# Transposed residual in two chunk places instead of four, one expert load in the room that this frees

## The chip, the cores and the metric

The kernel runs on one core of a Trainium2 chip. The metric is the time of one execution on the device in microseconds, as the median of several runs.

## The reference

One layer of a hybrid backbone for two streams of 128 tokens (context and latent), D = 2048, all in 32-bit floats. What matters here is its second half: the merged branches go through one output projection, the result is added to the residual (x1), the router's logits are taken from the normalised and modulated x1, and every token goes to the best 2 of 4 experts in its best of 4 groups.

```
x1 = x + ga1 * (merged @ w_out)                 # merged: sigmoid-gated sum of the two branches
h2 = rmsnorm(x1, norm2_g) * (1 + sc2) + sh2
lg, lf = h2 @ w_rg + b_rg, h2 @ w_re + b_re     # 4 group logits, 16 expert logits
# top group, then top 2 of its 4 experts, weights comb from the two softmaxes
for e in range(16):
    y = y + comb[:, e:e+1] * ((silu(h2 @ w_g[e]) * (h2 @ w_u[e])) @ w_d[e])
out = rmsnorm(x1 + ga2 * y, final_norm_g)
```

The weights are some 400 MB, and every byte of them is read once.

## The kernel before

The work is a row of stages on one core, each engine with its own hand-written program, synchronised by semaphores. In the dense stages a weight load of 1 MB (512 rows by 512 columns) goes into one of four slots `raw`; ScalarE rounds it into `w_hi` (`high`, L1362), VectorE takes the rest `w_lo` (`low`, L1719), and TensorE multiplies each of its two halves (`unit`, L812, 12 matmuls: two streams, two row blocks, three products). `w_hi` and `w_lo` hold four units (`AHEAD`, L32). A load is numbered l; loads L_OUT to L_ALL-1 (L344, L345, sixteen of them) are the output projection. It makes four column chunks of x1, numbered 24 to 27, with four loads each. A chunk's sums lie in banks 0 and 1 (chunks 25 and 27) or 2 and 3 (chunks 24 and 26; `banks_of`, L394).

When a chunk's last unit is used, VectorE reads it (`read_chunk`, L1810): for each stream a product with the gate (L1850) and a sum into `x1` (L1856). Behind the second product `step.settle()` waits for it, and only then is `chunk_read` raised (L1854); `reads(chunk)` (L399) is its value when that chunk has been read. TensorE transposes each stream's x1 columns (`x1_transposes`, L1010), stream 0 behind load l = L_OUT+4, +8, +12 and stream 1 in the middle of load +6, +10, +14; the last chunk's two come after the last load. ScalarE copies the transposed columns into `x1T` (`x1_transposed`, L1520), which has four chunk places, 16 KB in each partition. From it TensorE multiplies the router's weights (`router`, L1020, 4 products of 20 columns for one chunk and stream, which the profile shows as 8 matmuls at L1027); all of them sum into banks 2 and 3, so the first one waits until chunk 26 has been read (L1023). The products of chunk 0 stand in load L_ALL-3, those of chunk 1 in L_ALL-2, the others behind the last load (L1050 to L1079, L1098 to L1103).

The expert stage reads 1 MB pieces of the expert weights. SP issues them in a fixed order into a ring of eleven slots, eight of which lie where `w_hi`, `w_lo` and `raw` were; four more places are used once (loads 12 to 15, `slab`, L442). Two of these, `mraw_f[0]` and `mraw_f[1]` for loads 13 and 14, lie in the same 16 KB as `x1T`. So SP issues them only when all router products are done (`route_done`, L591). Before that SP issues loads 9, 10 and 8 at the start of the output projection, 15 when load L_ALL-3 has been used (L583), and 0, 2, 1, 3, 12 and 4 as the dense slots come free. From the second pair of experts on, each load waits until TensorE has used the slot (`slot_free`, L538, wait at L546). The first pair's gate and up loads are 0 to 15. During the output projection ScalarE's own queue issues the `w_out` loads (`dense_load`, L486, L499) and the last four loads of w_ada (L483).

Of the kernel before, what the change touches and what calls it, by code (L numbers as in the profile page):

```python
# [8 lines left out]
ACT = mybir.ActivationFunctionType  # L9
# [4 lines left out]
P = 128  # L14
TOK = 128
NS = 2
D = 2048
KD = D // P
# [6 lines left out]
NG, EPG, NE, EH = 4, 4, 16, 512  # L25
# [95 lines left out]
def backbone_step(nc, x_prompt, x_sample, cache_k, cache_v, c, c_ctx, norm1_g, norm2_g, w_ada, b_ada,  # L121
# [24 lines left out]
    with ExitStack() as ctx:  # L146
# [6 lines left out]
        def place(name, shape, offset, dt=F32):  # L153
            return nc.alloc_sbuf_tensor_at(name, shape, dt, offset=offset).ap()
# [8 lines left out]
        KB = 1024  # L163
# [9 lines left out]
        A, F, B = region(32 * KB), region(32 * KB), region(16 * KB)  # L173
# [13 lines left out]
        o_lo = place("o_lo", [P, KF, NS, TOK], F + 24 * KB, F32R)  # L187
        x1 = place("x1", [P, NS, D], F)
        ga2b = place("ga2b", [P, NS, D], F + 16 * KB)
        x1T = place("x1T", [P, KD, NS, TOK], F + 16 * KB)  # L190

        xg = place("xg", [P, KD, EPG * CAP], A)
        row_hi = place("row_hi", [P, COL], A + 14 * KB, F32R)
# [43 lines left out]
        gw = place("gw", [P, NS, KD, NG + NE], C + 4 * (C_DFTN + 384))  # L237
# [38 lines left out]
        bank = [ctx.enter_context(nc.psum_tensor(f"bank{i}", [P, COL], F32)) for i in range(8)]  # L276
# [7 lines left out]
        hi_ready, unit_used = sem("hi_ready"), sem("unit_used")  # L284
# [114 lines left out]
        def reads(chunk):  # L399

            return chunk + 1 + 3 * P0_CHUNKS

        def x1T_bank(n, s):

            return 4 + (2 * n + s) % 3
# [99 lines left out]
        @block.sync  # L505
        def _(sp):
            for s in range(NS):
                sp.dma_start(x0[:, s], x_v[s]).then_inc(x_in, 16)

            def ada_block_load(b, j):  # L510

                n = 8 * b + j
                if n >= ARAW:
                    sp.wait_ge(ada_done, n - ARAW + 1)
                for m in (SHIFT1, SCALE1):
                    sp.dma_start(araw[:, n % ARAW, 2 * m:2 * m + 2],
                                 ada_v[:, 2 * j:2 * j + 2, m * D + b * COL:m * D + (b + 1) * COL]).then_inc(part_landed[n % ARAW], 16)

            for j in range(8):
                ada_block_load(0, j)  # L520
            dense_load(sp, 0)
            for b in range(1, BLOCKS):
                for i in range(P0_CHUNKS):
                    if i < 4:
                        ada_block_load(b, 2 * i)
                        ada_block_load(b, 2 * i + 1)
                    dense_load(sp, P0_CHUNKS * (b - 1) + i + 1)
            for l in range(L_LOOP, SP_DENSE - 1):
                if l < L_LAST_ADA - LATE_ADA:
                    ada_super_load(sp, A_SUPER + l - L_LOOP)  # L530
                dense_load(sp, l + 1)

            def expert_load(n, view, row, col):

                sp.dma_start(slab(n).rearrange("p (a m) -> p a m", a=1),
                             view[:, row:row + 1, col:col + D]).then_inc(landed(n), 16)

            def slot_free(r, n):  # L538

                place = place_in_ring(n)  # L540
                if place >= MRAW:
                    sp.wait_ge(loads_used, used_value(r, load_at(place - MRAW)))
                else:
                    last = range(place, LOADS - ONCE, MRAW)[-1]
                    sp.wait_ge(loads_used, used_value(r - 1, load_at(last)))
                sp.sem_inc(slots_freed, 1)  # L546

            def gate_up_loads(r, i, q, up):
                for x in range(PAIR):
                    n = 2 * gate_up_unit(i, q, up) + x  # L550
                    slot_free(r, n)
                    expert_load(n, (gate_v, up_v)[up], i * PAIR + x, q * LOAD_K * COL)

            def down_loads(r, i):
                for k in range(KE):
                    for x in range(PAIR):
                        n = 2 * down_unit(i, k) + x
                        slot_free(r, n)
                        expert_load(n, down_v, (i * PAIR + x) * KE + k, 0)

            def last_down_loads(r):

                for q in range(D // COL):
                    for half in range(2):
                        n = 2 * down_unit(PAIRS - 1, q) + half
                        slot_free(r, n)
                        for x in range(PAIR):
                            row = ((PAIRS - 1) * PAIR + x) * KE + 2 * half
                            sp.dma_start(slab(n)[:, 2 * x * COL:(2 * x + 2) * COL].rearrange("p (k m) -> p k m", k=2),
                                         down_v[:, row:row + 2, q * COL:(q + 1) * COL]).then_inc(part_landed[2 * q + half], 16)  # L570

            rounds_end = sp.alloc_register("rounds_end")
            sp.reg_mov(rounds_end, 1)
            with sp.Fori(0, rounds_end) as r:

                def first_gate_up_load(n):
                    expert_load(n, (gate_v, up_v)[n // 2 % 2], n % 2, n // 4 * LOAD_K * COL)

                first_gate_up_load(9)
                first_gate_up_load(10)  # L580
                sp.wait_ge(chunk_read, reads(21))
                first_gate_up_load(8)
                sp.wait_ge(unit_used, 2 * L_ALL - 4)  # L583
                first_gate_up_load(15)
                for n in (0, 2, 1, 3):
                    sp.wait_ge(unit_used, 2 * L_ALL - 2 + n % 2 * 2)
                    first_gate_up_load(n)
                first_gate_up_load(12)
                sp.wait_ge(raw_done[0], 8 * (RING_LOADS // RAW))
                first_gate_up_load(RAW)  # L590
                sp.wait_ge(route_done, NS)  # L591
                first_gate_up_load(13)
                first_gate_up_load(14)
                for n in range(1, RAW):
                    sp.wait_ge(raw_done[n], 8 * (RING_LOADS // RAW))
                    first_gate_up_load(RAW + n)
                sp.wait_ge(rounds_ready, 1)
                sp.reg_load(rounds_end, rounds[0:1, 0:1])
                slot_free(r, 11)
                first_gate_up_load(11)  # L600
                for i in range(1, PAIRS):
                    for q in range(2):
                        for up in range(2):
                            gate_up_loads(r, i, q, up)
                    down_loads(r, i - 1)
                    for q in (2, 3):
                        for up in range(2):
                            gate_up_loads(r, i, q, up)
                last_down_loads(r)

                sp.wait_ge(x2_squared, r * 8 + 8)
                sp.sem_inc(slots_freed, 1)
                for place in range(MRAW):
                    slot_free(r + 1, load_at(place))

            sp.wait_ge(y_ready_act, 1)
            sp.dma_start(y_v[0][:, 0:2 * COL], x1[:, 0, 0:2 * COL]).then_inc(out_sent, 16)
            for s in range(NS):
                sp.wait_ge(y_ready, s + 1)
                sp.dma_start(y_v[s][:, 2 * COL:4 * COL], x1[:, s, 2 * COL:4 * COL]).then_inc(out_sent, 16)  # L620
            sp.wait_ge(out_sent, 16 * NS * 2)
            sp.wait_ge(kv_sent, 32)
# [159 lines left out]
        def _(pe):  # L782
# [237 lines left out]
            def router(n, s):  # L1020

                if n == 0:
                    pe.wait_ge(chunk_read, reads(26))  # L1023
                    pe.wait_ge(gw_ready, 1)
                pe.wait_ge(x1T_ready, 2 * n + s + 1)
                for k in range(4 * n, 4 * n + 4):
                    last = nc.tensor.matmul(bank[2 + s][:, 0:NG + NE], x1T[:, k, s], gw[:, s, k],  # L1027
                                            start=k == 0, stop=k == KD - 1)
                return last

# [7 lines left out]
            for l in range(L_LOOP, L_ALL - 1):  # L1038
# [8 lines left out]
                if l > L_LOOP:  # L1047
                    for a in supers_at(l):
                        ada_super(a)
                if l == L_ALL - 3:  # L1050
                    router(0, 0)
                if l == L_ALL - 2:
                    router(1, 0)
                for h in range(HEADS):
# [18 lines left out]
                        ada_super(a)  # L1073
                if l > L_OUT and l % 4 == 0:
                    x1_transposes((l - L_OUT) // 4 - 1, 0)
                if l == L_ALL - 3:
                    router(0, 1)
                if l == L_ALL - 2:
                    router(1, 1)  # L1079
                if l == ROUTER_AT + 2:  # L1080
# [279 lines left out]
        def _(act):  # L1360
# [158 lines left out]

            def x1_transposed(n, s):  # L1520
                act.wait_ge(x1T_done, 2 * n + s + 1)
                nc.scalar.activation(x1T[:, 4 * n:4 * n + 4, s], bank[x1T_bank(n, s)][:].rearrange("p (k t) -> p k t", k=4), ACT.Copy
                                     ).then_inc(x1T_ready, 1)

            def permuted(x, s, n):
# [779 lines left out]
```

## Time and profile before

| | us |
|---|---|
| median of 3 runs | 1196.16 |
| the runs | 1195.09 to 1196.16 |
| the profiled execution | 1196.65 |
| its span, first to last instruction | 1194.8 |
| TensorE busy in it | 1116.9 (93%) |
| VectorE busy | 535.9 (45%) |
| ScalarE busy | 366.3 (31%) |
| DMA, mean rate over the span | 354 GB/s |

A page of the profile gives the busy time of each engine, the span in 40 equal slices, and the chain of work that ended last. TensorE is busy 93% of the span, and 27% of the chain is DMA; both are means over stages with different limits, so the stretches of the stages that the change touches have to be read one by one. In the rows "PE" is TensorE, "DVE" VectorE, "ACT" ScalarE, "SP" the engine that issues most loads, and "PEclk" or the number behind the busy times the share of the full TensorE clock that was granted.

### The profile page before, as it was taken

The page shows a single profiled execution, that of the slowest core. Times are in us where ns is not written, and L with a number is a line of the kernel's source. Part 1 is how long each engine was busy: PE and PEld are TensorE (multiplying, and loading weights), DVE is VectorE, ACT ScalarE, POOL GpSimd, SP SyncE. Part 2 cuts the span into 40 slices and gives each one's busy share as a digit, 9 for nine tenths or more (in the row PEclk, how much of TensorE's full clock was granted, in tenths as well). Part 3 has the DMA queues.
Part 4 walks back from the last instruction along what each step waited for, and adds up shares of the span by engine and source line. Part 5 has one row for each costly group of instructions (what it writes and reads, how often), then busy time and mean ns, then how long its engine had stood idle before and what let it go on. Part 6 is the DMA issues. An engine that isn't in the chain of part 4 may idle for free.

```text
span 1194.8 us, 14481 instructions
## 1 busy us (share of the span) xinstructions
PE 1116.9 (93%) x5577; PEld 682.5 (57%) x5577; DVE 535.9 (45%) x781; ACT 366.3 (31%) x526; POOL 54.8 (5%) x100
## 2 busy tenths in 40 slices
PE   5899999999999999999999999999999888988795
PEld 2566766777777677667788875434344234423231
DVE  0464575555455444454466755242416041504056
ACT  3342342444433333333345533320112001201023
POOL 0210200110000220000010100000000000000000
PEclk9999999999999999999999999999999999999997
DMA  9999978887877898888898799999999999999994
GB/s 357 385 386 381 364 286 320 312 302 281 286 289 283 306 351 323 326 299 319 329 362 260 219 381 423 390 415 423 423 423 423 423 422 424 422 423 423 423 406 174
DMA packets 114964, 423.22 MB, mean 354 GB/s; under 512 B 9088, under 2 KB 9264, under 8 KB 82640
## 3 DMA queue, kind: packets, MB, share of 16 engines
q1 hardware_dynamic: 101968, 389.57, 83.4%
q0 software_dynamic: 5424, 15.35, 4.8%
q10 hardware_dynamic: 7504, 17.37, 4.0%
q8 instruction: 45, 0.74, 0.2%
q14 instruction: 23, 0.19, 0.0%
HBM read 418.27 MB, written 3.98 MB: 353 GB/s over the span
## 4 chain that ended last, share of the span: by engine, by line
PE 69%; DMA 27%; SPq 1%; DVE 1%; issue 1%; ACT 1%; DVEq 0%
PE bank L827 14%; PE bank L828 13%; PE bank L829 13%; PE bank L1196 10%; DMA mraw<-in_w_exp_up 10%; DMA mraw<-in_w_exp_down 5%; PE bank L808 5%; DMA raw<-in_w_in 4%; DMA mraw<-in_w_exp_gate 4%; PE bank L1235 3%; DMA raw<-in_w_ada 2%; PE bank L1135 2%; DMA mraw_y<-in_w_exp_gate 2%; PE bank L792 1%; PE bank L1277 1%; PE bank L1258 1%
## 5 line engine op out<-in xcount | busy, mean ns | idle before, releaser
L1724 DVE TENSOR_TENSOR w_lo<-raw,w_hi 128x1024 fp32r<-128x1024 f32 x192 | 231.8, 1223 | 246.7 <-ACT w_hi L1370 245.6
L1370 ACT ACTIVATE w_hi<-raw 128x1024 fp32r<-128x1024 f32 x192 | 200.3, 1057 | 313.3 <-DMA raw<-in_w_in 160.4
L827 PE MATMUL bank<-w_hi,h_hi 128*128 128x512 f32 x512 | 206.2, 403 | 6.6 <-DVE w_lo L1724 4.3
L828 PE MATMUL bank<-w_lo,h_hi 128*128 128x512 f32 x512 | 200.1, 391 | 0.0
L829 PE MATMUL bank<-w_hi,h_lo 128*128 128x512 f32 x512 | 199.8, 390 | 0.0
L1196 PE MATMUL bank<-mraw,xg 128*64 128x512 f32 x720 | 184.9, 597 | 12.5 <-DMA mraw<-in_w_exp_gate 4.8
L827 PEld LDWEIGHTS bank<-w_hi,h_hi 128*128 128x128 f32 x512 | 96.2, 188 | 47.1 <-issue 24.8
L1196 PEld LDWEIGHTS bank<-mraw,xg 128*64 128x64 f32 x720 | 57.7, 136 | 108.4 <-issue 105.6
L829 PEld LDWEIGHTS bank<-w_hi,h_lo 128*128 128x128 f32 x512 | 96.1, 188 | 21.0
L828 PEld LDWEIGHTS bank<-w_lo,h_hi 128*128 128x128 f32 x512 | 96.3, 188 | 18.1
L2190 DVE SCALAR_TENSOR_TENSOR d_lo<-bank,slot_w,d_hi 128x512 fp32r<-128x512 f32 x32 | 23.9, 747 | 161.6 <-ACT d_hi L1669 161.0
L1235 PE MATMUL bank<-mraw,hidT 128*64 128x512 f32 x336 | 84.3, 607 | 12.2 <-DMA mraw<-in_w_exp_down 12.2
L1669 ACT ACTIVATE d_hi<-bank,slot_w 128x512 fp32r<-128x512 f32 x32 | 22.0, 688 | 226.8 <-PE bank L1235 142.3
L2202 DVE TENSOR_TENSOR bank<-bank,ga2b 128x512 f32<-128x512 f32 x64 | 41.5, 694 | 77.1 <-PE bank L1277 77.0
L808 PE MATMUL bank<-raw,cpad 128*32 128x512 f32 x512 | 63.3, 610 | 2.8 <-DMA raw<-in_w_ada 2.8
L1235 PEld LDWEIGHTS bank<-mraw,hidT 128*64 128x64 f32 x336 | 26.9, 139 | 57.2 <-issue 52.7
L792 PE MATMUL bank<-araw,cpad 128*32 128x512 f32 x256 | 34.2, 643 | 14.8 <-DMA araw<-in_w_ada 14.8
L827 PE MATMUL bank<-w_hi,m_hi 128*128 128x512 f32 x120 | 47.7, 398 | 0.0
L829 PE MATMUL bank<-w_hi,m_lo 128*128 128x512 f32 x120 | 46.9, 390 | 0.0
L828 PE MATMUL bank<-w_lo,m_hi 128*128 128x512 f32 x120 | 46.7, 390 | 0.0
L2129 DVE TENSOR_TENSOR xg<-bank,rbi 128x512 f32<-128x512 f32 x32 | 21.9, 684 | 52.8 <-PE bank L1135 52.8
L1196 PE MATMUL bank<-mraw_g,xg 128*64 128x512 f32 x96 | 43.7, 598 | 1.6 <-DMA mraw_x<-in_w_exp_up 1.2
(293 smaller groups left out, 1332.2 us busy)
## 6 DMA issues: line engine op xcount, KB each, us to landing
raw<-in_w_in SPq DMA_DIRECT2D x64, 1024.0 KB, 8.3
raw<-in_w_ada SPq DMA_DIRECT2D x60, 1024.0 KB, 8.2
mraw<-in_w_exp_gate SPq DMA_DIRECT2D x46, 1024.0 KB, 20.8
mraw<-in_w_exp_up SPq DMA_DIRECT2D x44, 1024.0 KB, 20.9
mraw<-in_w_exp_down SPq DMA_DIRECT2D x42, 1024.0 KB, 20.6
araw<-in_w_ada SPq DMA_DIRECT2D x64, 512.0 KB, 10.9
raw<-in_w_out ACTq DMA_DIRECT2D x12, 1024.0 KB, 9.3
raw<-in_w_na_o SPq DMA_DIRECT2D x8, 1024.0 KB, 7.2
```

Source lines behind the costliest of these rows:

```text
L792: last = nc.tensor.matmul(bank[7 - b % 2][32 * g:32 * g + 32], cpad[:, 2 * j + g % 2], araw[:, n % ARAW, g], start=j == 0, stop=j == 7)
L808: last = nc.tensor.matmul(bank[7][32 * g:32 * g + 32], cpad[:, k], raw[:, n % RAW, g], start=k == 0, stop=k == KD - 1)
L827: nc.tensor.matmul(o, hi[:, k, s], wh, start=k == first, stop=False)
L828: nc.tensor.matmul(o, hi[:, k, s], wl, start=False, stop=False)
L829: last = nc.tensor.matmul(o, lo[:, k, s], wh, start=False, stop=k == final)
L1135: last = nc.tensor.matmul(out[:, kk * EPG * CAP:(kk + 1) * EPG * CAP], (t_hi, t_lo)[part][:, s, k * P:(k + 1) * P], pick[:, s, g * EPG:(g ...
L1196: last = nc.tensor.matmul(out[x * CAP:(x + 1) * CAP], xg[:, q * LOAD_K + kk, e * CAP:(e + 1) * CAP], slab(2 * unit + x)[:, kk * COL:(kk + ...
L1235: last = nc.tensor.matmul(bank[first_bank + n][x * CAP:(x + 1) * CAP], hidT[:, i % 2, k, x * CAP:(x + 1) * CAP], slab(2 * unit + x)[:, n * ...
L1370: nc.scalar.activation(w_hi[:, u % AHEAD], r, ACT.Copy).then_inc(hi_ready, 1)
L1724: v.tensor_tensor(w_lo[:, u % AHEAD], r, w_hi[:, u % AHEAD].bitcast(F32), ALU.subtract).then_inc(raw_done[n % RAW], 4)
L2190: v.scalar_tensor_tensor(out=d_lo[:, c % 2], in0=bank[first_bank + n][:], scalar=slot_w[:, i:i + 1], in1=d_hi[:, c % 2].bitcast(F32), op0= ...
L2202: v.tensor_tensor(bank[out + s][:], bank[out + s][:], ga2b[:, s, cols], ALU.mult).then_inc(y_scaled, 1)
```

## The change

`x1T` gets two chunk places instead of four. Chunk n uses place n mod 2, so chunk 2 goes where chunk 0 lay. The products of chunk 0 are therefore put one load earlier, into load L_ALL-4, both streams between that load's two units, in front of the transposes of chunk 2 behind the second unit. The freed 8 KB are the place of load 14; SP issues it behind two waits of its own (chunk 22 read, and unit 14 of the output projection used) before load 15, and no longer behind `route_done`.

```diff
@@ -187,7 +187,7 @@
         x1 = place("x1", [P, NS, D], F)
         ga2b = place("ga2b", [P, NS, D], F + 16 * KB)
-        x1T = place("x1T", [P, KD, NS, TOK], F + 16 * KB)
+        x1T = place("x1T", [P, 2 * 4, NS, TOK], F + 16 * KB)
@@ -580,6 +580,9 @@
                 first_gate_up_load(10)
                 sp.wait_ge(chunk_read, reads(21))
                 first_gate_up_load(8)
+                sp.wait_ge(chunk_read, reads(22))
+                sp.wait_ge(unit_used, 2 * L_OUT + 14)
+                first_gate_up_load(14)
                 sp.wait_ge(unit_used, 2 * L_ALL - 4)
                 first_gate_up_load(15)
@@ -590,7 +593,6 @@
                 first_gate_up_load(RAW)
                 sp.wait_ge(route_done, NS)
                 first_gate_up_load(13)
-                first_gate_up_load(14)
@@ -1024,7 +1026,7 @@
                 for k in range(4 * n, 4 * n + 4):
-                    last = nc.tensor.matmul(bank[2 + s][:, 0:NG + NE], x1T[:, k, s], gw[:, s, k],
+                    last = nc.tensor.matmul(bank[2 + s][:, 0:NG + NE], x1T[:, k % 8, s], gw[:, s, k],
                                             start=k == 0, stop=k == KD - 1)
@@ -1047,8 +1049,9 @@
-                if l == L_ALL - 3:
+                if l == L_ALL - 4:
                     router(0, 0)
+                    router(0, 1)
                 if l == L_ALL - 2:
                     router(1, 0)
@@ -1073,8 +1076,6 @@
                 if l > L_OUT and l % 4 == 0:
                     x1_transposes((l - L_OUT) // 4 - 1, 0)
-                if l == L_ALL - 3:
-                    router(0, 1)
                 if l == L_ALL - 2:
                     router(1, 1)
@@ -1519,7 +1520,7 @@
                 act.wait_ge(x1T_done, 2 * n + s + 1)
-                nc.scalar.activation(x1T[:, 4 * n:4 * n + 4, s], bank[x1T_bank(n, s)][:].rearrange("p (k t) -> p k t", k=4), ACT.Copy
+                nc.scalar.activation(x1T[:, n % 2 * 4:n % 2 * 4 + 4, s], bank[x1T_bank(n, s)][:].rearrange("p (k t) -> p k t", k=4), ACT.Copy
                                      ).then_inc(x1T_ready, 1)
```

## Rows read from the trace of the kernel before

**Rows 1.** Stretches: us, busy time (instructions) of each engine, PEclk, DMA share, GB/s.

```profile
680.00:690.00 10.00, 10.00 (x54) 8.43 (x52) 7.17 (x9) 4.71 (x8) 2.13 (x4) 1.00 0.65 171
690.00:715.00 25.00, 24.37 (x152) 18.13 (x151) 13.95 (x34) 9.42 (x19) 0.00 (x0) 0.93 1.00 403
...
757.00:760.00 3.00, 3.00 (x16) 1.01 (x14) 0.69 (x1) 1.24 (x2) 0.00 (x0) 1.00 0.76 259
...
774.00:778.00 4.00, 4.00 (x23) 1.82 (x24) 2.58 (x4) 0.00 (x0) 0.00 (x0) 1.00 0.88 289
...
782.00:830.00 48.00, 48.00 (x236) 19.98 (x234) 18.50 (x29) 8.20 (x16) 0.00 (x0) 1.00 1.01 423
830.00:1170.00 340.00, 303.57 (x1399) 122.08 (x1397) 105.19 (x166) 45.40 (x86) 0.00 (x0) 0.99 1.01 421
```

**Rows 2.** Waits of SP's queue, 715 to 782 us: total, times, longest.

```profile
SPq L546 <- PE bank L1196: 47.8, 10, 10.2
SPq L546 <- PE bank L1235: 7.2, 2, 4.7
```

**Rows 3.** Chain that ended last, in order of time: start, us, what.

```profile
686.10 0.80 PE bank L1027 x8
...
829.77 15.40 DMA mraw<-in_w_exp_up
```

**Rows 4.** SP's expert load issued at 778.5 us, alone, and its time to landing.

```profile
L535 SPq DMA_DIRECT2D mraw_x<-in_w_exp_up x1: 328/328/328, 778.5 to 778.5; - x1
...
DMA to landing us min/median/max: 6.2/6.2/6.2
```

**Rows 5.** Tile raw on ScalarE, 649.4 to 677.6 us; landings of its six loads.

```profile
L499 ACTq DMA_DIRECT2D raw<-in_w_out x5: 374/374/375, 649.3 to 672.1; - x5
L483 ACTq DMA_DIRECT2D raw<-in_w_ada x1: 353/353/353, 677.5 to 677.5; - x1
...
  PE bank L829: 14.1, 10
...
DMA to landing us min/median/max: 4.7/6.8/10.0
```

**Rows 6.** ScalarE in order of time: start, us, what [idle before, releaser].

```profile
663.47 1.06 ACT L1370 ACTIVATE w_hi<-raw 128x1024 fp32r<-128x1024 f32 x1 [0.77 <-PE bank L829]
```

**Rows 7.** TensorE in order of time, the first matmuls of both units of L_OUT+12.

```profile
677.30 0.39 PE L827 MATMUL bank<-w_hi,m_hi 128*128 128x512 f32 x1
...
680.02 0.39 PE L827 MATMUL bank<-w_hi,m_hi 128*128 128x512 f32 x1
```

**Rows 8.** VectorE in order of time, around the reading of chunk 26.

```profile
678.67 1.23 DVE L1724 TENSOR_TENSOR w_lo<-raw,w_hi 128x1024 fp32r<-128x1024 f32 x1 [1.44 <-ACT w_hi L1370]
...
681.13 0.68 DVE L1850 TENSOR_TENSOR gab<-gab,bank 128x512 f32<-128x512 f32 x1
681.96 0.69 DVE L1856 TENSOR_TENSOR x<-x,gab 128x512 f32<-128x512 f32 x1 [0.15 <-DVE gab L1850]
```

**Rows 9.** VectorE and TensorE in order of time, two handoffs between them.

```profile
71.97 1.23 DVE L1724 TENSOR_TENSOR w_lo<-raw,w_hi 128x1024 fp32r<-128x1024 f32 x1 [5.24 <-ACT w_hi L1370]
...
73.34 0.47 PE L827 MATMUL bank<-w_hi,h_hi 128*128 128x512 f32 x1 [1.22 <-DVE w_lo L1724]
...
715.09 0.70 PE L1146 MATMUL bank<-pick,rr 128*128 128x256 f32 x4 [0.71 <-DVE pick L2111]
```

**Rows 10.** TensorE in order of time, behind three pauses.

```profile
39.27 0.50 PE L827 MATMUL bank<-w_hi,h_hi 128*128 128x512 f32 x1 [2.17 <-DVE h_lo L1758]
...
1014.40 5.35 PE L1235 MATMUL bank<-mraw,hidT 128*64 128x512 f32 x16 [2.05 <-DMA mraw<-in_w_exp_down]
...
1069.48 3.65 PE L1235 MATMUL bank<-mraw,hidT 128*64 128x512 f32 x16 [1.41 <-DMA mraw<-in_w_exp_down]
```

**Rows 11.** TensorE's stretches: us, busy (matmuls), granted clock, DMA share, GB/s.

```profile
40.00:42.00 2.00, 2.00 (x10) 1.00 1.04 384
...
708.00:709.00 1.00, 1.00 (x7) 0.50 1.00 418
...
1015.00:1018.00 3.00, 3.00 (x10) 0.50 1.00 418
```

## The prediction, as it was made

> **What bounds the kernel now.** I read the stretches first, then each engine's order of time in the output stage, then the loads of the expert stage. The stretches [rows 1] show three regimes. Between 680 and 690 us TensorE is busy without a break while the DMA engines have room: 171 GB/s, against 421 to 423 GB/s where they are full. From 690 us they are nearly full, but TensorE still has hardly a gap. From 782 us to 1170 us the DMA engines stay at full rate and TensorE has holes (303.57 us busy of 340). So moving bytes forward helps only if the full-rate stretch begins or ends earlier.
>
> The stretch in between decides that. At 757 to 760 us and 774 to 778 us the rate falls to 259 and 289 GB/s [rows 1], although more than 380 us of transfers at full rate are still to come. The DMA queue's own waits say why [rows 2]: between 715 and 782 us it waits 47.8 us for L1196 and 7.2 us for L1235, TensorE's expert matmuls. All slots are full, and a load is issued only when TensorE has used up an old one. In the chain of waits the first link behind 686 us that is a transfer is issued at 829.77 us [rows 3]; it took 15.40 us because loads stood queued before it. The row to look at is the last load that found nearly nothing queued: issued at 778.5 us, landed 6.2 us later [rows 4]. After it the queue does not run dry again. So the end is set by when TensorE frees a slot at 778.5 us, plus a fixed amount of transfer. It is not set by how many loads were done before.
>
> **The change, part by part.**
>
> Load 14 forward. It leaves its place behind the routing and is issued when the units of the out projection's seventh load are used (`2 * L_OUT + 14`). One load is 1.05 MB, 2.48 us at 423 GB/s. If every byte in front of the end counted, this would be the gain. But the loads behind it then land 2.48 us earlier, the slots are full 2.48 us earlier, and the queue is dry for longer at 757 and 774 us, because the next issues still wait for TensorE. What is left of the gain is the part of the 6.2 us that the load of 778.5 us spent behind earlier ones. Of six loads of the same size on ScalarE's queue the fastest landed in 4.7 us [rows 5], so up to 6.2 - 4.7 = 1.5 us can be saved. Bounds: 0 (it stands behind just as much) and 2.48 us (C, below). I take 1.0 us, nearer to the full 1.5 because the queue will be drier than it was. The Trainium skill (DMA: Bandwidth & Descriptors, "Anatomy of one DMA") gives about 2.0 us fixed plus the bytes at 436 GB/s, for the GpSimd path: an estimate of 4.4 us for this load. No row here is as low; by it the saving would be up to 1.8 us and the sum 0.8 us lower.
>
> Load 14 in the output stage. Its 2.48 us run beside the w_out loads on ScalarE's queue. The slowest of those six landed in 10.0 us [rows 5]; even at 10.0 + 2.48 the one issued at 649.3 us would land at 661.8 us, and ScalarE reads that slot from 663.47 us [rows 6]. I take 0; without this cover the cost is at most 2.48 us. On SP's queue the two new waits stand in front of load 15 alone, which waits for a later unit anyway: 0. The issue that falls away behind the routing was no bottleneck, since the queue soon waits for slots [rows 2]: 0.
>
> x1T halved. The same eight copies and the same transposes: 0. Chunk 2 now goes where chunk 0 lay, and on TensorE, which works in order, the products of chunk 0 now stand before the transposes of chunk 2: no new wait there.
>
> The router products one load earlier. The two groups of eight small matmuls for chunk 0, 0.80 us each [rows 3], only move. But `router(0, 0)` waits at L1023 until chunk 26 is read out of banks 2 and 3. Today TensorE reaches it at 686.10 us, long after. Now both groups stand between the two units of load L_OUT+12 = L_ALL-4: the first begins at 677.30 us, the second at 680.02 us [rows 7]. VectorE reads chunk 26 [rows 8] right behind the `low` of 678.67 us; its second product runs from 681.13 to 681.81 us. The signal goes out behind `step.settle()`, and VectorE's next instruction starts at 681.96 us. From VectorE's end to TensorE's next matmul another handoff took 0.14 us (a `low` from 71.97 us for 1.23 us, the matmul at 73.34 us, [rows 9]). So TensorE stands still from 680.02 to about 682.10 us: 2.1 us. Bounds: 1.8 us (the wait ends with the product at 681.81) and 2.6 us (the slowest handoff near by left TensorE idle for 0.71 us, [rows 9]; 681.96 + 0.71 - 680.02). Queued behind it on TensorE is everything that follows: the second unit, the transposes of chunk 2, the last loads, the routing, the gathers. Nothing takes the pause up. TensorE has no gap there to give [rows 1], ScalarE is the one that waits for TensorE (14.1 us in ten waits, [rows 5]), and so does SP. So the slot of 778.5 us is freed 2.1 us later.
>
> The clock behind the pause. Before 1014.40 us TensorE idled 2.05 us. Soon after it resumed, the granted clock fell to 0.50, that is 1.2 GHz, and 16 matmuls took 5.35 us against 3.65 us at full clock, 1.70 us more [rows 10, 11]. A pause of 2.17 us before 39.27 us had no such result: 1.00 behind it [rows 10, 11]. So a pause of this length can go either way. Here the 2.1 us are followed at once by 1.6 us of products with 20 columns, and such light work does not hold the clock up: at 708 us it stood at 0.50 [rows 11] behind the last products. So I expect the fall. It would lie over dense units for the most part, so I price it like the row, +1.7 us, with bounds 0 and 1.7. The Trainium skill (TensorE: Matmul & The Clock Gate, "What's actually happening") says that a monitor halves the clock of an array that was lately idle. By that rule the sum is the one below, without it 1.7 us less; the row of 1014.40 us agrees, the row of 39.27 us does not.
>
> Sum: +2.1 + 1.7 - 1.0 = +2.8 us. The profiled execution took 1196.65 us (1194.8 us span, 1.85 us outside it); the median of the runs is 1196.16 us, 0.49 us lower. The terms are differences, so I add them to the median: **1199.0 us**, +0.23%.
>
> **The rivals.**
> A, the pause without the fall of the clock: +2.1 - 1.0 = +1.1, 1197.3 us. For it: the row of 39.27 us. Against: the pause and the light products together last 3.7 us.
> B, the forecast: 1199.0 us.
> C, the load is worth its full 2.48 us at the end because the queue behind 757 us is not really dry: 1195.8 us with the pause, 1197.5 us with the clock's fall too. For it: in the dips the rate is only some 35% down, so some DMA engines were behind others. Against: 6.2 us to landing.
> D, the other side, faster: no pause. If VectorE has read chunk 26 before TensorE arrives, only the load's gain is left: 1195.2 us at -1.0, 1193.7 us at the full -2.48. It decides if the product that ends at 681.81 us ends before 680.02 us, that is, if VectorE ran 1.8 us ahead. Against: the `low` in front of it waits for ScalarE [rows 8], and ScalarE for TensorE [rows 5], so VectorE cannot run ahead.
> That load 14 is not issued early at all would leave +2.1 or +3.8 us, inside B's and A's ranges; its wait is met five and a half loads before 680 us, at two units of 2.72 us each [rows 7] about 30 us, so it gets no chance of its own.
>
> **How the numbers follow.** Chances: B 0.60, A 0.24, C 0.10, D 0.06. B spans 1.8 + 1.7 - 1.5 to 2.6 + 1.7 - 0, so 1198.2 to 1200.5 us; A, likewise, 1196.5 to 1198.8 us. The range of 1196.3 to 1200.4 us holds both and the slower part of C; D and the rest of C are left out. A measurement of this kernel can tell about 0.2%, 2.4 us, from no change: below 1193.8 us is faster, above 1198.55 us slower. Faster is most of D: 0.05. Slower is B but for its lowest part, and a little of A: 0.57. The rest is 0.38.
>
> **What would show it.** Right: in the profile after, TensorE idles about 2 us before the first product at L1027, near 680 us, released by VectorE's L1850; load 14 is issued near 649 us; the dips of the DMA rate near 760 and 776 us are deeper; the load behind the second dip lands in about 5 us; the granted clock is 0.50 for some microseconds near 685 us (B) or not (A). Wrong: no idle time there (D), no dips behind 757 us (C), or a w_out load that lands later than ScalarE reads it.

## The result, and the profile after

The changed kernel took 1201.85 us (median of 5 runs, 1201.3 to 1202.3), against 1196.16 us (5 runs, 1195.09 to 1196.32) for the kernel before on the same chip: 1.0047 times, 95% interval 1.0033 to 1.0060, or 5.69 us more. The prediction said 1199.0 us with a range up to 1200.4 us. The direction was right; the size was twice what was forecast, and the time lies outside the range. The profiled execution took 1202.30 us (span 1200.5 us), 5.65 us above the one of before. Its lines are shifted by one or two (products L1029 for L1027, transposes L1019 for L1017, the units L829 to L831 for L827 to L829, VectorE's product L1851 for L1850), and its origin by 0.16 us: what lay at 680.02 us before lies at 680.18 us here if nothing has changed.

TensorE after, in order of time, from the end of the first unit of load L_OUT+12 on; start, us, what, idle before and its releaser (answers to [rows 3, 7]):

```profile
679.95 0.39 PE L831 MATMUL bank<-w_hi,m_lo 128*128 128x512 f32 x1
682.08 2.75 PE L1029 MATMUL bank<-gw,x1T 128*128 128x20 f32 x16 [1.74 <-DVEq L1855]
684.66 0.77 PE L829 MATMUL bank<-w_hi,m_hi 128*128 128x512 f32 x1
685.24 0.63 PE L830 MATMUL bank<-w_lo,m_hi 128*128 128x512 f32 x1
...
689.50 0.57 PE L831 MATMUL bank<-w_hi,m_lo 128*128 128x512 f32 x1
689.91 0.60 PE L1019 MATMUL bank<-cst_all,x 128*128 128x128 f32 x4
690.27 0.48 PE L829 MATMUL bank<-w_hi,m_hi 128*128 128x512 f32 x1
...
698.54 0.96 PE L1029 MATMUL bank<-gw,x1T 128*128 128x20 f32 x8
```

VectorE after, around the reading of chunk 26 (answers to [rows 8]):

```profile
680.68 0.69 DVE L1857 TENSOR_TENSOR x<-x,gab 128x512 f32<-128x512 f32 x1
681.29 0.68 DVE L1851 TENSOR_TENSOR gab<-gab,bank 128x512 f32<-128x512 f32 x1
682.12 0.69 DVE L1857 TENSOR_TENSOR x<-x,gab 128x512 f32<-128x512 f32 x1 [0.15 <-DVE gab L1851]
```

The pause is there, where it was predicted: TensorE stands until VectorE's second product has ended at 681.97 us. The slowing behind it was predicted too, but it is larger than the price that the prediction gave it. The 16 small products take 2.58 us to the start of the next matmul, against two groups of 0.80 us [rows 3]. The twelve matmuls of the second unit follow each other every 0.43 us, not 0.23 us, and fill 5.25 us, against the 2.72 us that a unit takes in [rows 7].

Stretches after, with the columns of [rows 1]:

```profile
680.00:690.00 10.00, 8.26 (x31) 6.67 (x30) 4.96 (x8) 1.06 (x1) 2.12 (x4) 0.66 0.70 164
...
757.00:760.00 3.00, 3.00 (x18) 0.95 (x16) 0.00 (x0) 0.53 (x2) 0.00 (x0) 1.00 1.00 421
...
774.00:778.00 4.00, 4.00 (x20) 1.34 (x19) 2.18 (x4) 3.24 (x7) 0.00 (x0) 1.00 1.00 414
778.00:782.00 4.00, 4.00 (x26) 2.58 (x28) 2.68 (x4) 0.00 (x0) 0.00 (x0) 1.00 0.88 336
```

The mean granted clock of 680 to 690 us is 0.66, where it was 1.00. The clock has two levels here, 1.00 and 0.50, so 0.34 below full means 2 * 0.34 * 10 = 6.8 us at 0.50, that is 1.2 GHz. Single microseconds show that it lay in one piece (TensorE alone: us, busy, granted clock, DMA share, GB/s; answers to [rows 11]), and the two last lines show that the first dip of the DMA rate has moved and is deeper than the 259 GB/s of [rows 1]:

```profile
683.00:684.00 1.00, 1.00 (x7) 0.53 0.00 0
686.00:687.00 1.00, 1.00 (x4) 0.50 1.07 180
689.00:690.00 1.00, 1.00 (x4) 0.56 0.99 164
...
761.00:764.00 3.00, 3.00 (x16) 1.00 0.29 120
764.00:774.00 10.00, 10.00 (x60) 1.00 0.99 398
```

The second dip has moved as well (336 GB/s at 778 to 782 us), but it is shallower than the 289 GB/s of [rows 1], against the sign that the prediction named.

The delay can be added up on TensorE. The first product of chunk 1 began in the kernel before, TensorE in order of time, at:

```profile
693.28 0.96 PE L1027 MATMUL bank<-gw,x1T 128*128 128x20 f32 x8
```

From 680.02 us to there it is 13.26 us, and after (680.18 to 698.54) it is 18.36 us, 5.10 us more, with the same work in between. The pause is 682.08 - 680.18 = 1.90 us of it. The products take 2.58 - 2 * 0.80 = 0.98 us more and the second unit 5.25 - 2.72 = 2.53 us more. The remaining -0.3 us is the difference in the rest of the stretch, where products no longer stand between the other units. These 5.10 us pass to the end as they are. SP's queue in order of time (start, us, what), the load of the slot that decides and the ninth load behind it, first of the kernel before:

```profile
778.50 0.33 SPq L535 DMA_DIRECT2D mraw_x<-in_w_exp_up  x1
...
792.75 0.33 SPq L535 DMA_DIRECT2D mraw<-in_w_exp_gate  x1
```

The same two of the kernel after:

```profile
783.69 0.33 SPq L535 DMA_DIRECT2D mraw_x<-in_w_exp_up  x1
...
797.93 0.33 SPq L535 DMA_DIRECT2D mraw<-in_w_exp_gate  x1
```

And each of the two of after read alone, with its time to landing (answer to [rows 4]):

```profile
L535 SPq DMA_DIRECT2D mraw_x<-in_w_exp_up x1: 328/328/328, 783.7 to 783.7; - x1
...
DMA to landing us min/median/max: 7.4/7.4/7.4
...
L535 SPq DMA_DIRECT2D mraw<-in_w_exp_gate x1: 328/328/328, 797.9 to 797.9; - x1
...
DMA to landing us min/median/max: 15.4/15.4/15.4
```

Without the shift of the origin the slot comes free 783.69 - 778.50 - 0.16 = 5.03 us later, the ninth load behind it is issued 5.02 us later, and takes 15.4 us to land in both kernels. The load of the slot itself took 7.4 us, not the 6.2 us of [rows 4], and not the 5 us that the prediction hoped for. The early load 14 has left nothing at this point.

### The profile page after: what moved, and what is told of

It is laid out like the page before. It is cut to its first block, busy times and chain, and to the rows that moved or that the text cites. A ratio compares the mean times of both kernels' runs of the same rounds, so it can differ in the third digit from the quotient of the medians.

```text
span 1200.5 us, 14482 instructions
## 1 busy us (share of the span) xinstructions
PE 1118.6 (93%) x5577; PEld 683.9 (57%) x5577; DVE 536.2 (45%) x781; ACT 366.3 (31%) x526; POOL 54.6 (5%) x100
## 4 chain that ended last, share of the span: by engine, by line
PE 69%; DMA 27%; DVE 1%; SPq 1%; issue 1%; ACT 1%; DVEq 0%
PE bank L829 14%; PE bank L830 13%; PE bank L831 13%; PE bank L1197 11%; DMA mraw<-in_w_exp_up 10%; PE bank L810 5%; DMA raw<-in_w_in 4%; DMA mraw<-in_w_exp_gate 3%; DMA mraw<-in_w_exp_down 3%; PE bank L1236 2%; PE bank L1136 2%; DMA raw<-in_w_ada 2%; DMA mraw_y<-in_w_exp_gate 2%; DMA araw<-in_w_ada 2%; PE bank L1278 1%; PE bank L794 1%
## 5 line engine op out<-in xcount | busy, mean ns | idle before, releaser
L829 PE MATMUL bank<-w_hi,h_hi 128*128 128x512 f32 x512 | 206.2, 403 | 7.7 <-DVE w_lo L1725 5.0
L831 PE MATMUL bank<-w_hi,h_lo 128*128 128x512 f32 x512 | 199.8, 390 | 0.0
L829 PEld LDWEIGHTS bank<-w_hi,h_hi 128*128 128x128 f32 x512 | 96.2, 188 | 48.2 <-issue 25.4
L831 PEld LDWEIGHTS bank<-w_hi,h_lo 128*128 128x128 f32 x512 | 96.1, 188 | 21.0
L829 PE MATMUL bank<-w_hi,m_hi 128*128 128x512 f32 x120 | 48.6, 405 | 0.0
L831 PE MATMUL bank<-w_hi,m_lo 128*128 128x512 f32 x120 | 47.7, 398 | 0.0
```

The source lines that it names most:

```text
L829: nc.tensor.matmul(o, hi[:, k, s], wh, start=k == first, stop=False)
L831: last = nc.tensor.matmul(o, lo[:, k, s], wh, start=False, stop=k == final)
```

## Experiments

All times are medians; the kernel before, run in between on the same chip, stood at 1196.2 us (e1 to e4), 1196.3 us (e5 to e8) and 1196.0 us (e9 to e11).

**e1: the early products without the pause.** Both groups of products move behind the second unit, directly ahead of the transposes of chunk 2, so that chunk 26 has been read when TensorE arrives.

```diff
-                if l == L_ALL - 4:
-                    router(0, 0)
-                    router(0, 1)
...
+                if l == L_ALL - 4:
+                    router(0, 0)
+                    router(0, 1)
```

> The changed kernel with both product groups of chunk 0 behind the second unit of load L_ALL-4, directly in front of the transposes of chunk 2. TensorE gets there at about 682.9 us, VectorE has read chunk 26 at about 682.0 us, so the pause should be gone. Theory (the time is pause plus half clock; the load forward is worth nothing at the end, since the end hangs on the slot freed near 778 us): 1196.2 us, between 1195.2 and 1197.0. Rival L (the load forward is worth its 2.48 us and something else costs the more): 1193.7 us. Rival T (load 14's traffic in the output stage costs the time): about 1201 us, as in the changed kernel.

1196.55 us (12 runs), 1.0002 times the kernel before (0.9993 to 1.0010). In its trace there is no pause and no fall of the clock at this place. TensorE in order of time:

```profile
682.09 1.85 PE L1029 MATMUL bank<-gw,x1T 128*128 128x20 f32 x16
```

The stretch around it, with the columns of [rows 1]:

```profile
680.00:690.00 10.00, 10.00 (x56) 8.59 (x56) 6.55 (x8) 4.20 (x8) 2.13 (x4) 1.00 0.58 170
```

The place of the products is the whole loss: 1201.85 - 1196.55 = 5.3 us. Everything else in the change, load 14 among it, nets to nothing within the interval.

**e2: load 14 back behind the routing,** everything else as changed.

```diff
-                sp.wait_ge(chunk_read, reads(22))
-                sp.wait_ge(unit_used, 2 * L_OUT + 14)
-                first_gate_up_load(14)
...
                 first_gate_up_load(13)
+                first_gate_up_load(14)
```

> The changed kernel with load 14 back behind the routing; x1T halved and the products early, as changed. Theory: the load's place is worth nothing at the end: 1201.8 us, as the changed kernel, within 0.7. Rival L (worth 2.48 us): 1204.3 us. Prediction's term (worth 1.0 us): 1202.8 us. Rival T (the load costs about 3 us where it is now): 1199 us.

1201.26 us, 1.0034 times (1.0021 to 1.0047): no later than with the early load. Pause and fall are those of the changed kernel (1.74 us idle, mean clock 0.66 from 680 to 690 us).

**e3: the pause filled.** Nine matmuls of 512 columns, about 2 us, into a free bank stand ahead of the products; TensorE reaches them as late as before, but has not idled. The nine results are not used.

```diff
                 if l == L_ALL - 4:
+                    for i in range(9):
+                        nc.tensor.matmul(bank[5][:].rearrange("p (k s t) -> p k s t", k=2, s=NS), m_hi[:, i, 0], m_hi[:, 4:6],
+                                         start=True, stop=True)
                     router(0, 0)
```

> The changed kernel with nine extra matmuls of 512 columns (9 x 0.227 = 2.05 us, into the free bank 5, never read) where TensorE waits for chunk 26. The wait is filled with dense work of the same length. Theory (idle time drew the clock down): granted clock 1.00 near 685 us, TensorE later by 2.0 us instead of 5.1, time 1198.2 us. Rival P (the light products alone draw it down): clock 0.50 for some time behind 683 us, 1199.9 us. Rival S (the shift has nothing to do with the clock): 1201.8 us.

1198.66 us, 1.0016 times (1.0006 to 1.0025). The products begin within 0.14 us of the changed kernel's, but take 1.86 us, and the clock stays up. TensorE in order of time, the nine matmuls, the products and the first product of chunk 1:

```profile
680.18 2.21 PE L1054 MATMUL bank<-m_hi 128*128 128x512 f32 x9
682.22 1.86 PE L1029 MATMUL bank<-gw,x1T 128*128 128x20 f32 x16
...
695.41 0.96 PE L1029 MATMUL bank<-gw,x1T 128*128 128x20 f32 x8
```

The stretch around it, with the columns of [rows 1]:

```profile
680.00:690.00 10.00, 10.00 (x56) 8.50 (x55) 6.20 (x9) 3.46 (x6) 2.13 (x4) 1.00 0.69 162
```

Nearly the same delay of the products, no fall: 1201.85 - 1198.66 = 3.2 us is the price of the fall. The traces agree: from the end of the first unit to the first product of chunk 1 it is 15.23 us here, against 13.26 us before and 18.36 us after, so the fall alone is worth 3.13 us on TensorE.

**e4: the pause alone.** The kernel before, with the wait for chunk 26 put between the two units of that load and the products left where they were.

```diff
+                if l == L_ALL - 4:
+                    pe.wait_ge(chunk_read, reads(26))
```

> The kernel before with one added wait: TensorE waits for chunk 26 between the two units of load L_ALL-4, and the products stay one load later, where they were; x1T whole, load 14 late. The pause is alone, dense units stand behind it. Theory: a pause of 1.9 us; if the clock holds 1198.1 us; if it falls, less long than the 6.8 us of the changed kernel, since dense work follows at once: 1199.8 us. Rival (products and pause have nothing to do with each other, the clock falls as long as before): 1201.5 us.

1198.82 us, 1.0021 times (1.0011 to 1.0031), so 1.3 to 3.7 us. TensorE idles as long as in the changed kernel, then dense units follow, and in its trace the clock does not fall here. TensorE in order of time, from the last matmul of the first unit to the first product of chunk 1:

```profile
679.58 0.39 PE L829 MATMUL bank<-w_hi,m_lo 128*128 128x512 f32 x1
681.70 0.50 PE L827 MATMUL bank<-w_hi,m_hi 128*128 128x512 f32 x1 [1.74 <-DVEq L1856]
...
695.11 0.96 PE L1027 MATMUL bank<-gw,x1T 128*128 128x20 f32 x8
```

The stretch around it, with the columns of [rows 1]:

```profile
680.00:690.00 10.00, 8.30 (x42) 7.01 (x43) 6.63 (x9) 4.51 (x7) 2.13 (x4) 1.00 0.50 140
```

Matmuls of a unit start 0.23 us apart, so the first unit ends at 679.81 us. Counted from there TensorE is 15.30 us away from chunk 1's products, 2.0 us more than before.

So neither the pause (e4) nor the light products (e1, e3) bring the clock down here. Both together do. Each of these is one trace: e1's is of a run of 1199.70 us, e4's of one of 1197.58 us, neither of them near its median. The mean granted clock that is on record for every run says the same: it averages 0.9928 over the 12 runs of e1, 0.9927 over the 12 of e3 and 0.9928 over the 11 of e4, as over 29 runs of the kernel before (0.9928), but 0.9898 over the five runs each of the changed kernel and of e2. By 2 * 0.0030 * 1200 that is 7.2 us at half clock, close to the 6.8 us of the trace.

**e5: one group of products between the units,** the other behind the second unit.

```diff
                 if l == L_ALL - 4:
                     router(0, 0)
-                    router(0, 1)
...
+                if l == L_ALL - 4:
+                    router(0, 1)
```

> The changed kernel with only the first product group of chunk 0 between the units (behind the wait for chunk 26) and the second one behind the second unit. The pause stays, the light work behind it is halved to 0.8 us. Theory (pause and light work together keep the clock down for 6.8 us): half clock shorter than in the changed kernel or absent; pause 1.9 plus 0 to 1.7: 1198.2 to 1199.9 us. Rival (any product behind the pause is enough): 1201.6 us, as the changed kernel.

1199.97 us, 1.0027 times (1.0013 to 1.0040). The same pause, half the light work behind it. TensorE in order of time:

```profile
681.97 1.07 PE L1029 MATMUL bank<-gw,x1T 128*128 128x20 f32 x8 [1.74 <-DVEq L1856]
```

The stretch around it, with the columns of [rows 1]:

```profile
680.00:690.00 10.00, 8.26 (x40) 6.86 (x40) 6.08 (x8) 3.45 (x6) 2.13 (x4) 0.83 0.67 159
```

A mean of 0.83 is 2 * 0.17 * 10 = 3.4 us at half clock, half of the changed kernel's 6.8 us. That is the length that the prediction had taken for two groups. It is one trace, and the nine runs lie between 1197.3 and 1202.7 us, where the five of the changed kernel lie within 1.0 us. That the length goes with the number of products is therefore not shown.

**e6: a load held back.** In the kernel before, load 15 is issued behind the routing, after 13 and 14, rather than when load L_ALL-3 has been used.

```diff
-                first_gate_up_load(15)
...
                 first_gate_up_load(14)
+                first_gate_up_load(15)
```

> The kernel before with one more load held back: load 15 is issued behind the routing, behind loads 13 and 14, and no longer when load L_ALL-3 is used. Between 690 and 710 us one load less moves (2.48 us). Theory (the end hangs on TensorE's slot near 778 us, the number of loads done before counts for nothing): 1196.2 us, or up to 1.3 us more if the dips at 757 and 774 us close. Rival L (every load in front counts): 1198.7 us.

1199.31 us, 1.0016 times (1.0006 to 1.0026): 0.7 to 3.1 us slower. The theory's plain case, no change, is out; its 1.3 us for closed dips and the rival's 2.5 us both lie in the interval. It is not the clock alone: among the runs with a mean granted clock of 0.993 or 0.994 six of e6 average 1198.0 us and nineteen of the kernel before 1196.0 us. In its trace the slots come free on the timetable of the kernel before (table below). But the ninth load behind the third slot, issued 73.1 us after the first expert matmul as in the kernel before, takes 1.3 us longer to land than the 15.4 us there:

```profile
L535 SPq DMA_DIRECT2D mraw<-in_w_exp_gate x1: 327/327/327, 795.0 to 795.0; - x1
...
DMA to landing us min/median/max: 16.7/16.7/16.7
```

So one load later costs something with the slots unmoved, while one load earlier (e1 against e11, below) gains nothing. It fits a queue that in the kernel before is just short of full in the dips, 259 and 289 GB/s [rows 1]; this reason for e6 is argued, not shown.

**e7 and e8: 2 us of matmuls in the expert stage.** Nine unused matmuls of 512 columns ahead of the second pair of experts (e7, near 754 us), or ahead of the fifth (e8, `i == 4`), in the stretch where the DMA engines are full.

```diff
+                    if i == 1 and q == 0 and up == 0:
+                        for j in range(9):
+                            nc.tensor.matmul(bank[2 * (i % 2)][:], t_hi[:, 0, j * P:(j + 1) * P], t_hi[:, 1, 0:COL],
+                                             start=True, stop=True)
```

> The kernel before with nine extra matmuls of 512 columns (2.05 us, into a bank that is about to be written anew, never read) in front of the second pair's first gate product, at about 754 us, in front of the last dry spells of the DMA queue. Theory (what TensorE loses in front of 778 us passes to the end in full): 1198.2 us. Rival (the end is set by the bytes to move): 1196.2 to 1196.7 us.

> The same nine extra matmuls in front of the fifth pair's first gate product, where the DMA queue never runs dry. Theory: hidden in TensorE's waits, 1196.2 us, within 0.6. Rival (TensorE's work passes to the end wherever it stands): 1198.2 us.

e7: 1199.59 us, 1.0028 times (1.0015 to 1.0041), so 1.8 to 4.9 us. e8: 1196.37 us, 0.9996 times (0.9986 to 1.0006). The same work costs its full length before 778 us and nothing behind it. TensorE's time up to the last slot that finds the queue nearly empty is what the end is made of, as long as no load comes later than in the kernel before (e6).

**e9 and e10: the slots freed sooner.** In the first pair of experts the transposes of the picks, the ga2 rows and the gathers for later pairs move behind matmuls that free slots. e9 is e1 with this order, e10 the kernel before with it. The core of the edit on TensorE (ScalarE's copies move along):

```diff
-                        pe.wait_ge(pick_ready, r * 2 + 2)
-                        pe.wait_ge(xg_scaled, r * 32 + 6)
...
-                ga2_rows(0)
-                ga2_rows(1)
...
+                        pick_transposes()
                     gate_up(i, 1, 0)
-                    next_group(i, 0)
+                    if i == 1:
+                        ga2_rows(0)
+                        ga2_rows(1)
+                    else:
+                        next_group(i, 0)
```

> The changed kernel with the products of chunk 0 behind the second unit of load L_ALL-4, and with another order in the first pair of experts: the transposes of the gathered picks and the ga2 rows stand behind the second pair's first gate and up products, so TensorE comes sooner to the matmuls that free the expert slots. Theory (the end is set by when TensorE frees the slots around 757 to 779 us, plus a fixed amount of transfer): the slots of 757.9, 772.8 and 778.5 us come free 2.1 to 3.4 us sooner, so 2.3 us less than 1196.2: about 1194.0. Rival (the DMA engines' bytes alone set the end, the slots do not): 1196.2, no change.

> The same other order in the first pair of experts, put into the kernel before (load 14 behind the routing, four places of x1T). Theory: 1.4 to 1.7 us less than 1196.2, about 1194.6, a little less than in the changed kernel, since with earlier slots the load that is already there counts for more. Rival (the slots do not set the end): 1196.2, no change.

e9: 1193.95 us (12 runs), 0.9981 times (0.9969 to 0.9993). e10: 1194.79 us (12 runs), 0.9984 times (0.9972 to 0.9997). Both are faster than both kernels, against the one before e9 by 2.0 us and e10 by 1.2 us. Counted from the first expert matmul of each trace, three slots come free at these times, and TensorE's last matmul starts at that in the last column:

| | first expert matmul at, us | slot 1 | slot 2 | slot 3 | last matmul |
|---|---|---|---|---|---|
| before | 719.66 | 38.26 | 53.15 | 58.84 | 461.74 |
| after | 724.86 | 38.26 | 53.14 | 58.83 | 462.20 |
| e6 | 721.90 | 38.26 | 53.14 | 58.83 | 462.93 |
| e7 | 718.82 | 40.51 | 55.39 | 61.09 | 464.26 |
| e9 | 718.47 | 35.74 | 49.75 | 57.84 | 459.95 |
| e10 | 721.80 | 35.74 | 49.74 | 57.84 | 461.42 |

(In the kernel before slot 1 is refilled at 757.92 us, slot 2 at 772.81 us, and slot 3 is that of [rows 4].) The changed kernel frees its slots on the same timetable as the one before, to 0.01 us; only its start is 5.20 us late (5.04 us without the shift of the origin). The last matmul is a blunter mark than the slots: in the ten traces with this timetable (before, after, e1 to e6, e8, e11) it lies between 461.74 and 463.06 us. e7 and e9 move the timetable, and TensorE's last matmul moves beyond that scatter: against the kernel before 2.5 us later (2.25 us of it already at the slots) and 1.8 us sooner. In e10 it moves by 0.3 us only, so its gain is shown by the times of its runs alone. Its trace is of a run of 1198.46 us. Among the runs with a mean granted clock of 0.993 or 0.994 ten of e9 and eight of e10 both average 1194.0 us, and eighteen of the kernel before 1195.8 us: the order is worth 1.8 us with either place of load 14. The third slot came 1.0 us sooner, not the 2.1 us of the estimate; the first two came as estimated.

**e11: e1 with load 14 behind the routing.**

```diff
-                sp.wait_ge(chunk_read, reads(22))
-                sp.wait_ge(unit_used, 2 * L_OUT + 14)
-                first_gate_up_load(14)
...
                 first_gate_up_load(13)
+                first_gate_up_load(14)
```

> The changed kernel with the products of chunk 0 behind the second unit of load L_ALL-4, as in e1, and with load 14 issued behind the routing again; what is left of the change is two places for x1T and products that stand a little earlier. Theory (load 14's early place is worth nothing while the slots are late): the same as e1, 1196.2 to 1196.6. Rival (load 14 early is worth 1.0 us or more, hidden in e1 by a cost of the products' new place): 1197.3 or more.

1196.42 us (12 runs), 0.9998 times (0.9987 to 1.0010), against 1196.55 us of e1. The early place of load 14 is worth nothing also where TensorE is not late.

## Why the prediction missed

| term | predicted, us | measured, us | by |
|---|---|---|---|
| pause | +2.1 (1.8 to 2.6) | +1.9 | the trace after; e4 is 2.6 slower in all |
| fall of the clock | +1.7 (0 to 1.7) | +3.2 to +3.5 | after against e3; products and unit at half clock |
| load 14 forward | -1.0 (-2.48 to 0) | 0 | e2 against after: 0.6 the other way; e11 against e1: 0.1 |
| sum | +2.8 | +5.7 | medians |

The measured terms make 5.1 to 5.4 us, and TensorE's first expert matmul comes 5.0 us later. The remaining 0.3 to 0.6 us are not put down to anything; they are less than the scatter of the last matmul.

**The pause** was right, in its place, releaser and size.

**The clock was the step that failed,** by its size. That it would fall, and why there (a pause followed by light products), was right, and e1, e3 and e4 show it: take away the idle time or the light products, and it does not fall here. But the sentence that such light work does not hold the clock up says too much: without the pause 16 products left it at 1.00 (e1, e3). The fall was priced like the row of 1014.40 us, as 1.7 us, and that value was made the upper bound too. But there dense matmuls followed the pause; here 1.6 us of 20-column products did, and they were slowed themselves. In the traces the fall had the length of that row with one group of them (e5, 3.4 us at half clock), and twice that with two (6.8 us, the changed kernel and e2). The dense unit that TensorE had meanwhile took nearly twice as long. The row of 1014.40 us was a sample of one, of another kind of work, so it could be no upper bound. Of the miss of 2.85 us this term is 1.5 to 1.8 us and load 14, below, 1.0 us. With twice its price as the bound the range would have reached about 1202.1 us and held the time.

The Trainium skill (TensorE: Matmul & The Clock Gate, "What's actually happening") puts the halving down to how busy the array was lately. e3 and e5 agree with it; the trace of e4, idle for the same 1.74 us without a fall, shows that such a pause alone is not enough at this place.

**Load 14** was the second error. The prediction itself argued that a load in front of a dry queue is worth nothing, and then took 1.0 us back for a shorter time to landing behind the second dip. In the first dip this came true: the load issued at 763.1 us into an almost empty queue landed in 4.7 us, not the 6.1 us of its counterpart (757.9 us before). This load of after, read alone:

```profile
L535 SPq DMA_DIRECT2D mraw<-in_w_exp_down x1: 327/327/327, 763.1 to 763.1; - x1
...
DMA to landing us min/median/max: 4.7/4.7/4.7
```

That is the value of the fastest of [rows 5]. The Trainium skill (DMA: Bandwidth & Descriptors, "Anatomy of one DMA") makes an estimate of 4.4 us for it, by a fit for the GpSimd path; the measured 4.7 us decides. But the queue was not empty at the second dip: eight slots later the same load as in [rows 4] took 7.4 us. The gain of the first dip is used up by the next slot that TensorE has yet to free. Why this load took 1.2 us longer than before is not settled. Load 14 is not the reason, for in e2, with load 14 back behind the routing, it took 7.2 us too. At the ninth load behind it the difference is gone.

**The cover in the output stage** held: load 14 was issued at 649.55 us, and no wait of ScalarE's `high` grew; the six `raw` loads beside it landed in 4.7 to 9.9 us, against 4.7 to 10.0 us in [rows 5]. Tile raw on ScalarE's queue after:

```profile
L499 ACTq DMA_DIRECT2D raw<-in_w_out x5: 374/375/408, 649.5 to 672.2; - x5
...
  PE bank L831: 14.1, 10
...
DMA to landing us min/median/max: 4.7/7.5/9.9
```

**What bounds the kernel** was read rightly for TensorE's part, and e7 to e9 show it: the end follows TensorE's timetable up to the slots of 758 to 779 us. That the number of loads done before does not count held for a load moved forward (e2, e11), and not for one held back (e6). **Rivals.** C (the load worth its 2.48 us) fell by e2 and e11, D (no pause) by the trace after. A (no fall) fell for this kernel; e3 stands in for it, at 1198.66 us with the load gain at 0.

## What to carry over

A wait put between two dense stretches cost more than its idle time here, where the first thing behind it was light work: put the light work where its inputs are already there (e1, 5.3 us), or dense work first (in e4's trace the clock held). Price a clock fall by what runs behind the pause, and do not take the one example that a trace has for its upper bound: here it was twice that. Before moving a load forward, ask which engine frees the place of the next load: here TensorE's order of freeing the slots set the end, and reordering TensorE's work by which slot it frees gained 2.0 us (e9), where the load gained none.

## What had not been expected of the hardware

The clock also falls near 707 us, behind the last router products, and there its length differs from run to run of much the same code. TensorE alone from 700 to 720 us, with the columns of [rows 11], in the trace of before:

```profile
700.00:720.00 20.00, 19.29 (x135) 0.91 1.00 403
```

In that of e1:

```profile
700.00:720.00 20.00, 20.00 (x119) 0.74 1.00 410
```

In that of e9:

```profile
700.00:720.00 20.00, 18.77 (x140) 1.00 1.01 424
```

That is about 3.5 us, 10 us and nothing at half clock. Of the thirteen traces five have none there (e4, e5, e7, e9, e11), five have about 3.5 us (before, after, e2, e3, e8) and three about 10 us (e1, e6, e10). What sets the length there was not tried.

A pause in front of dense work is no surer. The one near 39 us [rows 10], 2.17 us with no fall in the kernel before, stands in code that no experiment touches. In the trace of e8 it lasted 2.59 us and the clock was down behind it, in that of the changed kernel 2.64 us and the clock held. First e8, TensorE in order of time and its stretch with the columns of [rows 11]:

```profile
39.37 0.79 PE L827 MATMUL bank<-w_hi,h_hi 128*128 128x512 f32 x1 [2.59 <-DVE h_lo L1762]
...
40.00:41.00 1.00, 1.00 (x4) 0.50 1.07 393
```

The same of the kernel after:

```profile
39.36 0.50 PE L829 MATMUL bank<-w_hi,h_hi 128*128 128x512 f32 x1 [2.64 <-DVE h_lo L1759]
...
40.00:41.00 1.00, 1.00 (x6) 1.00 1.06 389
```

Such falls are a good part of the scatter of 1 to 6.5 us in the runs of one kernel: the nine runs of e1 with a mean granted clock of 0.993 or more average 1196.1 us, the three below it 1198.7 us. So single profiles of these kernels can't be compared to a microsecond. Medians of a dozen runs can be compared within the interval given with them, and so can slots that are counted from a common event within a trace; they agree to 0.01 us, the last matmul to 1.3 us.
